# Last projection of a two-layer backbone computed inside the recurrent layer's block, in two passes over halves of its contraction

## The reference, cut to what matters

```python
def _odd_mixer(u_lat, u_ctx, ...):
    z = u_lat @ w_in                       # 4096 columns: 2048 of x, 2048 of the gate z
    x_l = _dwconv(z[..., :W_RNN], conv_w, left) + conv_b
    ...
    a_l, b_l = _rglru_coeffs(x_l, w_ra, b_ra, w_ri, b_ri, lam)   # two gates per direction, blocks of 256
    _, y_l = _bidir_scan(a_l, b_l, h_ctx_T)                      # h = a*h + b, forward and backward
    y_lat = (y_l * silu(z[..., W_RNN:])) @ w_out                 # (1024 x 2048) @ (2048 x 1024)

h_lat = h_lat + gate * y_lat
return h_lat * rsqrt(mean(h_lat**2) + EPS) * final_g
```

## Time and profile before

| what | before |
|---|---|
| median of 3 runs (2362.93 to 2363.29) | 2362.94 us |
| span of the profiled execution | 2356.9 us |
| median less span (what lies around it) | 6.0 us |
| TensorE matmul busy | 2252.5 us, 96% of the span |
| VectorE, ScalarE, GpSimd busy | 64%, 51%, 21% |
| mean granted TensorE clock | 0.983 of full speed |
| read from and written to HBM | 166 MB and 32 MB, 84 GB/s |

### The profile page before, as it was taken

The page is one execution under the profiler, slowest core; times in us unless marked ns, Lnnn a source line. Parts: engine busy times, 40 slices in busy tenths (PEclk is TensorE's granted clock), DMA queues, the critical chain, the costliest instruction groups (busy, mean ns, idle before and its releaser), DMA issues. The chain is left out here.

```text
span 2356.9 us, 33916 instructions
## 1 busy us (share of the span) xinstructions
PE 2252.5 (96%) x12000; PEld 1959.2 (83%) x12000; DVE 1497.3 (64%) x2375; ACT 1190.8 (51%) x1720; POOL 505.3 (21%) x296
## 2 busy tenths in 40 slices
PE   6999999999999999999997999799999999995998
PEld 4788888888888888888885888689999999994887
DVE  4576675766757667576686347557866786677444
ACT  4534445344353454534444234276787678767322
POOL 0232232322313223133221200112122222220300
PEclk9999999999999999999998999899999999997999
DMA  7111221112211122111107556111111111114654
GB/s 288 45 56 41 67 60 64 55 49 65 61 64 53 51 65 62 63 53 51 56 27 267 151 164 181 42 36 56 56 60 45 60 57 54 45 54 160 205 161 143
DMA packets 165414, 200.04 MB, mean 85 GB/s; under 512 B 51096, under 2 KB 125976, under 8 KB 162200
## 3 DMA queue, kind: packets, MB, share of 16 engines
q1 hardware_dynamic: 155336, 174.53, 23.7%
q10 hardware_dynamic: 9792, 23.07, 2.8%
q0 software_dynamic: 144, 0.52, 0.1%
HBM read 166.11 MB, written 31.98 MB: 84 GB/s over the span
## 5 line engine op out<-in xcount | busy, mean ns | idle before, releaser
L958 PE MATMUL ps<-u_hi,w_hi 128*128 128x512 f32 (+1 forms) x1464 | 533.7, 365 | 0.0
L958 PE MATMUL ps<-u_hi,w_lo 128*128 128x512 f32 (+1 forms) x1464 | 519.0, 355 | 0.0
L958 PE MATMUL ps<-u_lo,w_hi 128*128 128x512 f32 (+1 forms) x1464 | 517.8, 354 | 0.0
L958 PEld LDWEIGHTS ps<-u_hi,w_lo 128*128 128x128 f32 x1464 | 276.2, 189 | 40.1
L958 PEld LDWEIGHTS ps<-u_lo,w_hi 128*128 128x128 f32 x1464 | 277.0, 189 | 35.0
L958 PEld LDWEIGHTS ps<-u_hi,w_hi 128*128 128x128 f32 x1464 | 276.4, 189 | 35.0
L1650 POOL TENSOR_TENSOR o_w_lo<-o_w_raw,o_w_hi 128x1024 fp32r<-128x1024 f32 x48 | 133.6, 2783 | 664.7 <-ACT o_w_hi L1665 664.7
L1924 PE MATMUL ps<-u_hi,o_w_hi 128*128 128x426 f32 (+2 forms) x640 | 237.2, 371 | 10.3 <-POOL o_w_lo L1650 9.3
L573 ACT ACTIVATE probs<-probs,neg_max 128x640 f32<-128x640 f32 (+1 forms) x160 | 122.8, 768 | 244.4 <-DVE neg_max L774 244.4
L1924 PE MATMUL ps<-u_lo,o_w_hi 128*128 128x426 f32 (+2 forms) x640 | 237.2, 371 | 0.0
L1924 PE MATMUL ps<-u_hi,o_w_lo 128*128 128x426 f32 (+2 forms) x640 | 237.2, 371 | 0.0
(11 more groups left out here) (192 smaller groups left out, 4384.7 us busy)
## 6 DMA issues: line engine op xcount, KB each, us to landing
y_tile<-y_scratch SPq DMA_DIRECT2D x72, 512.0 KB, 5.1
w_stage<-in_w_even SPq DMA_DIRECT2D x63, 512.0 KB, 3.8
o_w_raw<-in_w_odd SPq DMA_DIRECT2D x48, 512.0 KB, 3.7
ada_piece<-in_w_ada SPq DMA_DIRECT2D x20, 1024.0 KB, 5.7
wout_raw<-in_w_out SPq DMA_DIRECT2D x16, 1024.0 KB, 9.6
y_scratch<-h_backward SPq DMA_DIRECT2D x16, 512.0 KB, 2.6
h_scratch<-h_tile ACTq DMA_DIRECT2D x18, 256.0 KB, 2.3
h_tile<-h_scratch ACTq DMA_DIRECT2D x18, 256.0 KB, 3.0
```

The lines of the kernel that those rows point to most:

```text
L958: last = nc.tensor.matmul(ps[:, bank(j, g), 0:t - f], w[:, slot, c * P:(c + 1) * P], x[:, c, f:t], start=(c == 0 and n == 0), stop=(c == K ...
```

## The change

The fourth stage goes, and its work moves into `odd_layer`'s block, so that no barrier lies between them. It is divided differently. Pass 0 now covers the first eight y chunks (first half of the contraction) for all 1024 columns, pass 1 the other eight. A tile of a pass is again 48 matmuls: 8 chunks x 2 column halves x 3. The partial result of pass 0 is multiplied by the gate row and added to the residual stream, which now stays in SBUF for all eight tiles. Pass 1 adds its part there, and the norm follows.

The gate row for all 1024 columns is made once, at the start of `odd_layer`: GpSimd sets the ones, VectorE makes the diagonals, TensorE multiplies them, ScalarE copies the row.

In the last block, TensorE computes `Z1`'s second group ahead of the gates of recurrence 1. ScalarE takes the root of recurrence 0 and `Z1`'s second Tanh ahead of those gates. SyncE loads y tile 0, four weight pieces and y tile 1 after that group, the residual stream after the last gates, y tile 2 after the store of the first chunk, and y tile 3 and the rest after the store of the second. VectorE copies pass 0's weights to hi in eight units: two ahead of recurrence 1, four inside it behind its first product, two behind it. It makes y tile 0's lo in recurrence 1, tile 1's in recurrence 2 and tile 2's behind recurrence 3. GpSimd makes the eight lo units. Pass 1's weights are split by ScalarE and GpSimd during pass 0. There are two y buffers, and lo replaces the raw tile in place, so a y tile is loaded when the tile two before it has been multiplied.

The diff, without allocations, semaphores and the small steps of the norm:

```diff
@@ -165,7 +164,6 @@
         even_layer(**env)
         out_projection(layer=0, **env)
         odd_layer(**env)
-        out_projection(layer=1, **env)
 
 
 BG, CC, CX, CB, CG, CQ, CK, CV = range(8)
...
@@ -1631,17 +1668,49 @@
                     load(n + 1, X1)
                 else:
                     sp.wait_ge(proj, unit(n, Z1, 1) + 1)
-                    for q in range(4):
-                        load_wout(sp, a, k, 1, 0, q, k["wout_raw"][1])
+                    for mm in range(2):
+                        sp.wait_ge(y_stored[mm], 16 * n)
+                    load_y(0, 0)
+                    for r in range(4):
+                        load_final_w(0, r)
+                    load_y(0, 1)
+                    sp.wait_ge(gate_mm, 24 * BLOCKS)
+                    sp.wait_ge(conv_done, 2 * BLOCKS)
+                    for q in range(2):
+                        sp.dma_start(hq[q][:].rearrange("p t a n -> p t (a n)"),
+                                     dram["h1"][4 * q:4 * q + 4].rearrange("t p d -> p t d")).then_inc(h_loaded[q], 16)
                 store(n, 0)
+                if last:
+                    load_y(0, 2)
                 if not last:
                     for j in (Z0, GW0, Z1, GW1):
                         load(n + 1, j)
                 store(n, 1)
 
+            def load_y(pass_, t):
+
+                q = pass_ * NLT + t
+                if q >= 2:
+                    sp.wait_ge(f_mm, 2 * (q - 1))
+                sp.dma_start(fyraw[:, q % 2], dram["y1"][KC * pass_:KC * pass_ + KC, :, t * P:(t + 1) * P].rearrange("c p n -> p c n")
+                             ).then_inc(fy_loaded[q % 2], 16)
+
+            def load_final_w(pass_, r):
+
+                sp.dma_start(fraw[pass_][:, r], a["w_out1"][:, 4 * pass_ + r].rearrange("h p m -> p h m")
+                             ).then_inc(fw_loaded[r], 16)
+
             run(sp, prologue, body)
+            load_y(0, 3)
             for mm in range(2):
                 sp.wait_ge(y_stored[mm], 16 * BLOCKS)
+            for r in range(4):
+                load_final_w(1, r)
+            sp.dma_start(fg[:], a["final_g"].partition_broadcast(P)).then_inc(fg_loaded, 16)
+            for t in range(4, NLT):
+                load_y(0, t)
+            for t in range(NLT):
+                load_y(1, t)
 
...
+            def final_lo(pass_, u):
+
+                pool.wait_ge(fw_hi, 8 * pass_ + u + 1)
+                nc.gpsimd.tensor_tensor(flo[pass_][:, u // 2, u % 2], fraw[pass_][:, u // 2, u % 2],
+                                        fhi[pass_][:, u // 2, u % 2].bitcast(F32), ALU.subtract).then_inc(fw_lo, 1)
+
+            def prologue():
+                nc.gpsimd.memset(ones[:], 1.0).then_inc(ones_set, 1)
+                split_lo(0, 0)
+
+            run(pool, prologue, body)
+            for pass_ in range(2):
+                for u in range(8):
+                    final_lo(pass_, u)
 
...
+                act.wait_ge(row_mm, 1)
+                nc.scalar.activation(grow[:], ps[:, 2:4, :], ACT.Copy).then_inc(row_done, 1)
...
@@ -1752,18 +1836,26 @@
                 decay(n, 0)
                 split_hi(n, GW1)
                 tanh_z(n, Z1, 0)
-                gate_units(n, 1, 0)
-                root(n, 0)
+                if last:
+                    root(n, 0)
+                    tanh_z(n, Z1, 1)
+                    gate_units(n, 1, 0)
+                else:
+                    gate_units(n, 1, 0)
+                    root(n, 0)
                 gate_units(n, 1, 1)
                 decay(n, 1)
-                tanh_z(n, Z1, 1)
-                if not last:
+                if last:
+                    final_y_hi(0)
+                else:
+                    tanh_z(n, Z1, 1)
                     split_hi(n, X0)
                 gate_units(n, 2, 0)
                 root(n, 1)
                 gate_units(n, 2, 1)
                 decay(n, 2)
                 if last:
+                    final_y_hi(1)
                     gate_units(n, 3, 0)
                     root(n, 2)
                 else:
...
+            def final_y_hi(q):
+
+                act.wait_ge(fy_loaded[q % 2], 16 * (q // 2 + 1))
+                if q >= 2:
+                    act.wait_ge(f_mm, 2 * (q - 1))
+                nc.scalar.activation(fyhi[:, q % 2], fyraw[:, q % 2], ACT.Copy).then_inc(fy_hi, 1)
+
+            def final_w_hi(u):
+
+                act.wait_ge(fw_loaded[u // 2], 32)
+                nc.scalar.activation(fhi[1][:, u // 2, u % 2], fraw[1][:, u // 2, u % 2], ACT.Copy).then_inc(fw_hi, 1)
...
+            def finish(t):
+
+                for half in range(2):
+                    act.wait_ge(f_h, 2 * (NLT + t) + half + 1)
+                    if 2 * t + half:
+                        act.wait_ge(squared, 2 * t + half)
+                    nc.scalar.activation(junk[:], h_of(t)[:, half], ACT.Square, accum_out=ss[:, t, half:half + 1]
+                                         ).then_inc(squared, 1)
+                act.wait_ge(var_done, t + 1)
+                nc.scalar.activation(rms[:, t:t + 1], var[:, t:t + 1], ACT.Sqrt).then_inc(rooted, 1)
...
             run(act, prologue, body)
+            final_y_hi(2)
+            final_y_hi(3)
+            for u in range(4):
+                final_w_hi(u)
+            final_y_hi(4)
+            for u in range(4, 8):
+                final_w_hi(u)
+            for q in range(5, NLT + 3):
+                final_y_hi(q)
+            for t in range(NLT):
+                if t + 3 < NLT:
+                    final_y_hi(NLT + t + 3)
+                finish(t)
+                store_out(t)
+            act.wait_ge(stored, 16 * NLT)
...
+            def recur(n, p, link, aside=None, before=None):
 
                 s = p % 2
                 dve.wait_ge(gate_read, n * 24 + (6 * p + 3) + 6)
                 link(nc.vector.scalar_tensor_tensor(out=B[:, s, :], in0=B[:, s, :], scalar=1.0, in1=xc[:, p % 2, :],
                                                     op0=ALU.add, op1=ALU.mult))
+                if before:
+                    before()
                 dve.wait_ge(th_done, n * 4 + (p + 1))
...
+                for c in range(KC):
+                    ins = nc.vector.tensor_scalar(diag[:, c * P:(c + 1) * P], k["ident"][:], k["modx"][:, 24 + c, 0:1], None,
+                                                  ALU.mult)
+                ins.then_inc(diag_done, 1)
...
-                recur(n, 1, link, lambda: silu_z(n, Z1, 1))
-                recur(n, 2, link)
+                if last:
+                    silu_z(n, Z1, 1)
+                    final_w_hi(0)
+                    final_w_hi(1)
+                    recur(n, 1, link, lambda: final_y_lo(0), lambda: [final_w_hi(u) for u in range(2, 6)])
+                    final_w_hi(6)
+                    final_w_hi(7)
+                    recur(n, 2, link, lambda: final_y_lo(1))
+                else:
+                    recur(n, 1, link, lambda: silu_z(n, Z1, 1))
+                    recur(n, 2, link)
                 add_streams(n, 0, link)
...
+                else:
+                    final_y_lo(2)
                 add_streams(n, 1, link)
                 gate_streams(1)
...
+            def final_w_hi(u):
+
+                dve.wait_ge(fw_loaded[u // 2], 16)
+                nc.vector.tensor_copy(fhi[0][:, u // 2, u % 2], fraw[0][:, u // 2, u % 2]).then_inc(fw_hi, 1)
+
+            def final_y_lo(q):
+
+                dve.wait_ge(fy_hi, q + 1)
+                nc.vector.tensor_tensor(fylo[:, q % 2], fyraw[:, q % 2], fyhi[:, q % 2].bitcast(F32),
+                                        ALU.subtract).then_inc(fy_lo, 1)
+
+            def add_half(pass_, t, h, link):
+
+                v = 2 * (pass_ * NLT + t) + h
+                dve.wait_ge(f_mm, v + 1)
+                if pass_ == 0 and h == 0 and t % 4 == 0:
+                    dve.wait_ge(h_loaded[t // 4], 16)
+                if v >= 2:
+                    dve.wait_ge(f_h, v - 1)
+                link(nc.vector.tensor_tensor(tmp[:, h], ps[:, v % 8], grow[:, 512 * h:512 * h + 512], ALU.mult))
+                nc.vector.tensor_tensor(h_of(t)[:, h], h_of(t)[:, h], tmp[:, h], ALU.add).then_inc(f_h, 1)
+
...
+                nc.vector.scalar_tensor_tensor(out=at, in0=at, scalar=rinv[:, c], in1=fg[:],
+                                               op0=ALU.mult, op1=ALU.mult).then_inc(normed, 1)
...
+            link = Link(dve, f_link)
+            dve.wait_ge(row_done, 1)
+            for pass_ in range(2):
+                for t in range(NLT):
+                    q = pass_ * NLT + t
+                    add_half(pass_, t, 0, link)
+                    add_half(pass_, t, 1, link)
+                    if 3 <= q + 3 < 2 * NLT:
+                        final_y_lo(q + 3)
+                    if pass_:
+                        normalise(t, link)
...
+            def final(pass_, t):
+
+                q = pass_ * NLT + t
+                bank_of = [(2 * q + h) % 8 for h in range(2)]
```

(54 more changed lines are left out.)

43 lines of the change are left out of this document (42 added, 1 removed).

## The result

Changed kernel: 2349.52 us (median of 4, 2348.12 to 2350.65); the kernel before, run beside it: 2362.93 us. The ratio is 0.9944, 95% interval 0.9931 to 0.9957, so 13.4 us faster. Forecast were 2347.4 us and a gain of 15.5. The profiled execution took 2349.3 us with a span of 2347.5. Run once more, they gave 2351.33 and 2361.59 (0.9952, 0.9938 to 0.9966).

A forecast was written before the change was run, and what follows sets the result against it. Bound: TensorE idle 33 us between stages. Stalls of 19.2 us and matmuls of 174.2 us give -17.8, tail +1.9, layer's start +0.4: -15.5; span 2341.4 plus 6.0 makes 2347.4 us, range 2335 to 2358.

The forecast's parts named there:

- layer's start: Gate row made ahead of the layer's first projection: between +0.3 and +2.2 us, taken as 0.4.
- stall in the fourth gates: Last block: TensorE waits 10.8 us for a bank, behind VectorE's late product of recurrence 1.
- ahead of tiles 1, 2, 4: Projection: TensorE waits 3.2 us for bank reads, 3.3 for y_lo 2, 1.9 for y tile 4's load and split.
- tail: From last matmul to span's end: 10.4 us instead of 8.5, as VectorE's last rounds run late.
- around the span: Time outside the profiled span: 6.0 us, the median less the span, added to the forecast span.
- the hold: Last block: each weight difference on GpSimd shuts VectorE out for some 2.2 us.
- costly term: Last block: VectorE's copies and GpSimd's differences shut each other out and alternate, delaying recurrence 1's product; without shutting out, -13.9 us.
- 0.2268 a matmul for all 768: Both projection passes: 768 matmuls at 0.2268 us each, 174.2 us in all.
- The clock after tile 4's stall: Restart at the lower clock after the 1.9 us stall ahead of tile 4: bounded at 0 to +1.9 us.
- Rival 1: Last block: engines hardly shut each other out; stall in the fourth gates 1.4 us, time 2333.5; chance 0.13.
- Rival 2: The stall only moves: unhidden waits reach 30 us instead of 19.2, time 2358 to 2366; chance 0.08.
- Rival 3: Projection from tile 4 on: y tiles set the pace, up to 3.6 us a tile, time 2390; chance 0.04.

The follow-up runs named there:

- four edits: Changed kernel with pass 0's differences on VectorE, y tile 4 loaded first, second-pass weights 384 bytes further, gate row's products inside the last fourth gates: 2336.16 us.
- fifth edit: Added to the four edits: in the second pass, normalisation goes ahead of a later tile's y split, taken two tiles on instead of three: 2335.13 us.
- tiny-differences one: Changed kernel with GpSimd's eight pass 0 weight differences cut to 8 of 1024 columns, same matmuls: 2336.63 us, ratio 0.9892 to the kernel before.
- copies-behind run: Changed kernel with VectorE's weight copies 2 to 5 moved behind recurrence 1's product with the root's argument: 2350.88 us, ratio 0.9954 to the kernel before.

## Why the prediction came out, and which terms were wrong

The mechanism was right in the last block: the hole of 33 us went, VectorE and GpSimd shut each other out, L1963 was late by it, and three of the four stalls stood where forecast. At the layer's start and in the second pass's matmuls it was not. Sizes, the profile after beside the prediction's terms:

| term | predicted | measured |
|---|---|---|
| layer's start | +0.4 | +3.6 in this pair of profiles, 2.5 over 13 |
| stall in the fourth gates | 10.8 | 9.8 |
| ahead of tiles 1, 2, 4 | 3.2, 3.3, 1.9 | 0, 3.0, 3.0 (second trace 0.7, 3.0, 1.1) |
| from the first stall to tile 4's start | 66.3 | 66.3 |
| tile 4's start to the last matmul | 130.6 | 135.0 |
| tail | 10.4 | 8.5 |
| around the span | 6.0 | 1.8 |

**What held.** From 2137.72 to 2204.03 the changed kernel takes 66.31 us, and 2200.0 - 2133.7 is 66.3. Up to tile 2's start, which hangs on VectorE, it takes 41.26 us against 42.6 (2176.3 - 2133.7); from there to tile 4's, which hangs on its load of 11.45 us, 25.05 against 23.7. That the first is near comes of VectorE's order, worked out step by step; that the two misses cancel is luck. The copies' price, 0.75 from the nearest row, was 0.69, and the hold, 2.2, was 2.1. Tile 1's stall went because the rest of the fourth gates ran at the lower clock, 6.4 us (2147.53 to 2153.96) instead of 3.5: the prediction had the restart vanish in that stall, at 1.9 us. The rows (columns as above):

```profile
2148.00:2154.00 6.00, 6.00 (x19) 5.58 (x19) 5.93 (x6) 5.97 (x6) 1.29 (x1) 0.52 0.00 0
2154.00:2160.00 6.00, 6.00 (x28) 4.98 (x27) 5.97 (x2) 2.42 (x4) 5.09 (x2) 1.00 0.77 285
```

**Layer's start.** The step failed in leaving GpSimd out of it. The diagonals were given 1.89 us from the earlier trace rows, a stretch in which GpSimd took no such difference; here its split of the first weights runs, and the lock that the prediction's costly term was built on applied here as well. So the first matmul came at 1509.65, 1.0 us later than before, where 1.5 sooner was forecast. The clock didn't make that good: the granted clock was 0.50 from 1510 to 1515, against 0.83 in the trace of before (in the second trace of before, whose first matmul comes at 1510.70, it was 0.50 too).

**0.2268 a matmul for all 768.** Right for the first pass, 0.2332 in the second: +2.5 us, from an address that stands in the diff and was not weighed. The prediction named another pitch as a sign that it would be wrong, and this sign came.

**The clock after tile 4's stall.** Bounded 0 to 1.9 and taken as 0; 1.7 in one trace, hidden in the other.

**Tail.** 2 us too long, because the second pass was slower than forecast and VectorE caught up in it, and because VectorE's round takes 6.2 us instead of 6.45 (6.19 from 2318.09 to 2324.28, with four edits). With the offset mended it grew to 9.3, and the fifth edit removed what the prediction described (a split of tile 15 in front of a normalisation).

**Around the span.** 6.0 was the wrong reading: 1.8 lie around it, and the other 4.2 were a quick execution. The figure still served, since it carried the forecast from a quick execution to a usual one. By medians the change was -13.4 against -15.5: the row (+2.1) and the pitch (+2.5), less the tail (1.9) make +2.7 where 2.1 differ; what is left is inside the interval, which is 6 us wide. That misses of either sign left only 2.1 us is in part luck. The two profiles alone would have said 9.4.

**Rivals.** Rival 1 was not this kernel but is the tiny-differences one, within 2 us of its price. Rival 2 (the stall only moves) has its mechanism in the copies-behind run, not its size. Rival 3's y tiles held single tiles (4, and 5 when 4 went first) for 0.4 to 3 us, never every tile.

## What to carry to other kernels

Before work is handed to an idle engine, ask what the two share: a difference that GpSimd did in VectorE's place held VectorE longer than VectorE needed to do it. When a stall is worked out, work out the order of the engine behind it, not the stall: moving the stalled instruction forward only moved the wait. Check a moved step against everything else that runs at its new place, and compare medians, not two profiles.

## What the hardware showed unexpectedly

Weights whose SBUF address in bytes leaves 256 when divided by 512 took 0.2332 us a matmul of 512 fp32 columns, those that leave 128 took 0.2266, all three products alike; no other offset was tried. Whether a stall of 3.0 us is followed by the lower clock differed between executions of one kernel: in one trace the clock stayed up after the stall ahead of tile 2 and fell after tile 4's, at a cost of 1.7 us, in the other it fell after tile 2's. From the last matmul ahead of the layer to the first gates, 9.3 to 9.4 us of them without a matmul, the same instructions on TensorE took 50.8 to 52.4 us in five traces.
